# One product of the v projection cut into token pieces in three retention heads, and a scalar projection with 64 weight columns

## What is computed

```python
h = rmsnorm(x, norm_mix_w[i])
# layer 0: four retention heads and four gated-delta heads in parallel
rq, rk, rv, rg, qkv, gz, ga, gb = _split(h @ w_in, HYB_SIZES)
rv = sw(rv.astype(jnp.float32).reshape(Bsz, L, RET_HEADS, RET_DV))
ro, ret_s = ret_fn(rq, rk, rv, log_gamma, ret_s0)
g = -jnp.exp(a_log) * jax.nn.softplus(ga + dt_bias)
beta = jax.nn.sigmoid(gb)
go, gdn_s = gdn_fn(gq, gk, gv, sw(g), sw(beta), gdn_s0)
x = x + mixed @ w_out
# layer 1: a Mamba-2 state-space mixer; each layer is followed by a SwiGLU
x = x + swiglu(rmsnorm(x, norm_ffn_w[i]), wg, wu, wd)
```

## Time and profile before

| | |
|---|---|
| three runs | 3317.96, 3323.27, 3329.45 us |
| median | 3323.27 us |
| span of the profiled execution | 3317.2 us |
| TensorE busy, matmul / weight load | 3143.7 us (95%) / 3030.1 us (91%), 20090 of each |
| DVE, ScalarE, GpSimd busy | 1775.8, 799.8, 1019.1 us |
| mean granted TensorE clock | 0.986 of full speed |

### The profile page before, as it was taken

The page is one execution under the profiler, slowest core; times in us unless marked ns, Lnnn a source line. Parts: engine busy times, 40 slices in busy tenths (PEclk is TensorE's granted clock), DMA queues, the critical chain, the costliest instruction groups (busy, mean ns, idle before and its releaser), DMA issues. The chain is left out here.

```text
span 3317.2 us, 46817 instructions
## 1 busy us (share of the span) xinstructions
PE 3143.7 (95%) x20090; PEld 3030.1 (91%) x20090; DVE 1775.8 (54%) x2023; ACT 799.8 (24%) x1176; POOL 1019.1 (31%) x528
## 2 busy tenths in 40 slices
PE   6999899998899999999989998999988999999997
PEld 5899898888799999999988897989978999999997
DVE  5344657566543333333487869678696333333335
ACT  4222414324420000000145415243253000000002
POOL 2222201111023333333334536345362333333331
PEclk9999999999899999999999999999999999999999
DMA  4111100101011111111113214132231111111111
GB/s 147 59 71 59 49 26 33 40 26 40 21 44 45 50 46 45 45 51 45 45 42 121 86 58 148 62 118 74 82 128 37 51 45 45 50 47 45 46 51 64
DMA packets 94474, 198.15 MB, mean 60 GB/s; under 512 B 21796, under 2 KB 52164, under 8 KB 94152
## 3 DMA queue, kind: packets, MB, share of 16 engines
q1 hardware_dynamic: 52384, 150.03, 12.9%
q10 hardware_dynamic: 41896, 45.23, 4.3%
HBM read 171.41 MB, written 19.59 MB: 58 GB/s over the span
## 5 line engine op out<-in xcount | busy, mean ns | idle before, releaser
L492 POOL CAST w_hi<-w_raw 128x1024 fp32r<-128x1024 f32 x230 | 256.8, 1116 | 2181.2 <-PE ps_set L565 1971.5
L565 PE MATMUL ps_set<-h_hi,w_hi 128*128 128x344 f32 x3648 | 806.0, 329 | 2.2 <-DVE work L2179 1.3
L565 PE MATMUL ps_set<-h_lo,w_hi 128*128 128x344 f32 x3648 | 776.8, 321 | 0.0
L565 PE MATMUL ps_set<-h_hi,w_lo 128*128 128x344 f32 x3648 | 772.0, 320 | 0.0
L565 PEld LDWEIGHTS ps_set<-h_hi,w_hi 128*128 128x128 f32 x3648 | 615.5, 189 | 26.8 <-issue 18.7
L565 PEld LDWEIGHTS ps_set<-h_lo,w_hi 128*128 128x128 f32 x3648 | 619.9, 190 | 0.0
L565 PEld LDWEIGHTS ps_set<-h_hi,w_lo 128*128 128x128 f32 x3648 | 610.6, 188 | 0.0
L495 POOL TENSOR_TENSOR w_lo<-w_raw,w_hi 128x1024 fp32r<-128x1024 f32 x230 | 599.0, 2605 | 18.4
L1824 DVE TENSOR_TENSOR x<-x,ps_set 128x1032 f32<-128x1032 f32 x160 | 196.7, 1229 | 255.6 <-PE ps_set L565 255.6
L1131 ACT ACTIVATE work<-work 128x1032 f32<-128x1032 f32 (+5 forms) x190 | 180.7, 959 | 496.0 <-DVE work L2179 447.9
L565 PE MATMUL ps_set<-y_hi,w_hi 128*128 128x344 f32 x1296 | 282.7, 327 | 8.5 <-DVE y_lo L2360 7.0
(11 more groups left out here) (229 smaller groups left out, 3652.7 us busy)
## 6 DMA issues: line engine op xcount, KB each, us to landing
w_raw<-in_w SPq DMA_DIRECT2D x230, 512.0 KB, 3.2
work<-ssm_cum_rows ACTq DMA_DIRECT2D x32, 512.0 KB, 4.8
sample<-in_ssm_state SPq DMA_DIRECT2D x16, 512.0 KB, 5.1
out_ssm_s<-sample SPq DMA_DIRECT2D x16, 512.0 KB, 2.8
x<-in_x SPq DMA_DIRECT2D x6, 688.0 KB, 15.5
work<-work ACTq DMA_DIRECT2D x16, 258.0 KB, 2.4
out_y<-x SPq DMA_DIRECT2D x6, 688.0 KB, 3.4
sample<-bc_rows SPq DMA_DIRECT2D x8, 512.0 KB, 4.7
```

The source lines that it names most:

```text
L492: return nc.gpsimd.tensor_copy(w_hi[:, k, :], w_raw[:, k, :])
L565: mm = nc.tensor.matmul(out[:, g, 0:TN], w[:, slot, cols], v[:, g * TN:(g + 1) * TN], start=(start and n == 0), stop=(stop and n == 2))
```

## The change

`split_products` gets two arguments: `m`, the number of weight columns loaded (and of output partitions written), and `cuts`, the ends of the pieces into which each token group of the second product (`n == 1`, high weight x low activation) is cut. `slices` and `tile` pass them on. The v projection is called with other cuts for each head: head 0 with the whole 344, head 1 with 258 and 86 tokens, head 2 with 172 and 172, head 3 with 86 and 258. The scalar projection of layer 0 is called with `m` = 64. All other calls keep their 128 columns and one piece.

```diff
-            def split_products(out, slot, block, rhs, start, stop):
+            def split_products(out, slot, block, rhs, start, stop, m=P, cuts=(TN,)):
 
                 hi, lo = rhs
-                cols = slice(block * P, block * P + P)
+                cols = slice(block * P, block * P + m)
                 for n, (w, v) in enumerate(((w_hi, hi), (w_hi, lo), (w_lo, hi))):
                     for g in range(TG):
-                        mm = nc.tensor.matmul(out[:, g, 0:TN], w[:, slot, cols], v[:, g * TN:(g + 1) * TN],
-                                              start=(start and n == 0), stop=(stop and n == 2))
+                        first = 0
+                        for last in cuts if n == 1 else (TN,):
+                            mm = nc.tensor.matmul(out[0:m, g, first:last], w[:, slot, cols], v[:, g * TN + first:g * TN + last],
+                                                  start=(start and n == 0), stop=(stop and n == 2))
+                            first = last
                 return mm
...
-                fill(project("v", h), KC)
+                fill(slices(big_, f"v.{h}", 0, RET_UNIT["v", h], RET_UNIT["v", h], P, ((TN,), (258, TN), (172, TN), (86, TN))[h]), KC)
...
-            tile(big_jobs["gdns"], "sc", 0, GDNS, GDNS)
+            tile(big_jobs["gdns"], "sc", 0, GDNS, GDNS, 64)
```

More of the change, by code:

```diff
@@ L628, in pair_outputs, with slices @@
                 mm.then_inc(*((unit_done, 1) if done else (part_done, 1)))
-            def slices(jobs, job, turn, unit, slot):
+            def slices(jobs, job, turn, unit, slot, m=P, cuts=(TN,)):
                 part = take(jobs, job, turn)
@@ L636, in slices @@
                 for c in range(KC):
-                    mm = split_products(ps_set[part], slot % 2, c, (h_hi[:, c, :], h_lo[:, c, :]), c == 0, c == KC - 1)
+                    mm = split_products(ps_set[part], slot % 2, c, (h_hi[:, c, :], h_lo[:, c, :]), c == 0, c == KC - 1, m, cuts)
                     if c == KC - 1:
@@ L640, in slices, with tile @@
                     yield
-            def tile(jobs, job, turn, unit, slot):
-                for _ in slices(jobs, job, turn, unit, slot):
+            def tile(jobs, job, turn, unit, slot, m=P):
+                for _ in slices(jobs, job, turn, unit, slot, m):
                     pass
```

## The result

The changed kernel takes 3327.89 us (median of 20 runs, 3322.65 to 3336.48), the kernel before 3323.01 us beside it (20 runs, 3315.6 to 3329.45). The ratio is 1.0016, with a 95% interval of 1.0009 to 1.0023: 4.9 us slower by the medians and 5.3 us by the ratio (interval 3.0 to 7.6 us), where 5.3 us were forecast. It is within 0.3%, and clear of zero only because of the twenty runs.

What follows compares the result with a forecast made beforehand. TensorE was taken to bound the kernel, with matmuls under way 95% of the span. Splits of 1.85 + 1.63 + 1.85 = 5.3 us plus zero for the scalar projection took the median 3323.27 to 3328.6 us; range 3318 to 3339.

Steps and rivals of the forecast that it cites:

- the three stretches: v projections of heads 1, 2 and 3, 72 matmuls each: forecast to last 13.2, 13.0, 13.2 us instead of 11.4.
- The windows in which the prediction looked: The last 11.4 us before 142.5, 217.5 and 292.5 us, taken as v of heads 1 to 3, TensorE full.
- The count: v of heads 1 to 3: 24 further matmuls and 24 further loads a head, 72 in all, same moving columns.
- The floor of 113 ns: Short v pieces: each costs at least 113 ns, set by the load of 128 weight columns.
- the surcharge: 14.5 ns above the pure stream of 143.3 ns for 344 columns, added to each piece's streaming time.
- the prediction's own sign: v of heads 1 and 3: equal stretches would show that the order of long and short pieces means nothing.
- The scalar projection: 72 matmuls loading 64 weight columns: priced at zero, at most 1.0 us of gain or loss.
- Pieces at the float32 rate: Rival at the v pieces: 86 columns cost 228 ns, 172 cost 292 ns; 19.4 us slower together, chance 0.09.
- The fixed price of 157.8 ns: Rival at the v pieces: every float32r matmul takes 157.8 ns however few its columns; 11.4 us slower, chance 0.07.
- No floor: Rival at the v pieces: the second load hides or is left out, 1.0 us remains, 3324.3 us; chance 0.10.
- The clock: Rival: shifted low-clock stretches give over 10 us gain, chance 0.03; clock falling inside v stretches, up to 34 us, chance 0.01.
- nothing absorbs it: After v in heads 1 to 3: no later wait takes up the 5.3 us, so all of it reaches the path.

Runs made afterwards that it cites:

- v_quarters: The changed kernel with the second product of v in heads 1 and 3 cut into four 86-column pieces: 3338.51 us against 3322.38 before, ratio 1.0053.
- v_half_loads: The changed kernel with all v projections loading 64 weight columns, upper 64 rows omitted: v stretches 11.30, 11.82, 11.35, 11.76 us (heads 0 to 3), one execution.

## Why the prediction was right

**The bound and the place.** TensorE set the end, and in the three stretches nothing else was near. The 5.13 us that the stretches grew by are the 4.9 us of the medians within the interval (3.0 to 7.6 us). The windows in which the prediction looked were about 1.3 us late: v of head 1 runs from 129.80 to 141.17, and what follows up to 142.5 is the slice of the g projection, likewise in heads 2 and 3. TensorE is as full in one as in the other, so nothing hung on it. The DVE rotation that the k transposes need was ready as early as foreseen; the row after that answers to the earlier trace rows has the last operation at 214.49, and the transposes at 222.2.

```profile
214.49 1.23 DVE L1892 TENSOR_TENSOR work<-work 128x1032 f32<-128x1032 f32 x1
```

**The count** of 72 matmuls and 72 loads is in the page.

**The price.** The floor of 113 ns, read from float32 rows of 1 and of 128 columns, holds for float32r too: 112 ns in v_quarters. The forecast of 77, 68 and 77 ns a split stands against 77, 65 and 72. The small miss is in the surcharge, which the prediction added as 14.5 ns to every piece whatever its width, where nearly all of it goes with the columns. By 0.459 ns a column (157.8 ns for 344) the 258-column piece is 118 ns, not 122, and 118 + 112 - 158 = 72 ns is what head 3 shows. For 172 columns nothing changes by it; with 112 ns for the floor and 158 for the whole the sum is 66, measured 65. That head 1 agrees with its forecast is partly luck, since that forecast has the same 4 ns too much in it. By the prediction's own sign the order of a long and a short piece means something: head 1, with its long piece ahead, pays 5 ns more a split than head 3. Why was not tried.

**No slack is passed on.** The prediction took the larger of stream and load for each piece and added then, without a reason; adding first and comparing then would have given another price. The runs bear it out. The pieces of head 3 stream for 39 + 118 ns, together the 158 of the whole, and their two loads take 224; had the long piece made good what the short one lacks, a split would cost 224 - 158 = 66 ns there as in head 2. It costs 72. The single starts in the trace show where the wait falls: from an 86-column piece to the start of the next 258-column one it is only 40 ns, and from that to the next 190, which is its own 118 and the 72 that the short one lacked.

**The scalar projection** was priced at zero between +1.0 and -1.0 us. It gave 0.13 to 0.15 us (11.30 and 11.28 us against 11.43): about 0.1 us by 1.2 to 1.4 ns a matmul, and the rest in the first slice.

**The rivals.** Pieces at the float32 rate would have shown 290 ns a piece of 172 columns; head 2's have 112 (a slice of 1.62 us), and so have the pieces of 86 in v_quarters, where the prediction's rival had 228. The fixed price of 157.8 ns falls with the same rows. No floor falls with the 5.1 us; what would take the floor away is shorter loads, as v_half_loads shows. The Trainium skill's rule for the isolated distance, columns / 2.4 + 2.5 ns ("TensorE: Matmul & The Clock Gate", section "Back-to-back issue gap"), would give 38 ns for 86 columns; they took 112 with full loads and 58 with half, and the section itself says that in a stream of loads and matmuls the spacing is set by both. Its section "LDWEIGHTS", columns / 1.2, gives 107 and 53 ns for a load. The distances from start to start agree to about 5 ns; the durations of the load rows, 190 and 135 ns, do not.

**The clock** did move low stretches about, worth 5.1 us in the state-space stage of a single profile, and nothing in the medians beyond their interval.

**One step that held for this place only.** The prediction's "nothing absorbs it" was argued from the waits of the three heads. Where TensorE has waits that a longer projection can fill it doesn't hold: a quarter of the price did not show in the state-space stage (20.5 of 83.2 us).

No experiment pointed to a version faster than before that computes the whole result: the load is already hidden under 344 columns, and the narrow load gives 0.15 us where it can be had.

## What to carry to other kernels

A matmul costs the larger of its stream and of the load of its weights, and here each one loads anew, even with the same weights. Take the larger for each matmul and add then: a long neighbour does not make good what a short one lacks. For 128 columns the load is 112 ns, that is the stream of about 245 columns of float32r at 2.4 GHz; cut no piece shorter than that unless it loads fewer columns too. Read what a short matmul costs over a whole slice, not from the row it stands in, since its wait falls behind its successor. An isolated count times such a floor is a good price only where TensorE hardly waits; in a stage where it waits for other engines between its projections, part of the price disappears.

## What was not expected of the hardware

The float32r stream runs at 0.459 ns a column at the upper clock, 10% above 0.417, nearly in proportion to the width (157 ns for 344, 80 for 172), and without the surplus at the lower clock. Less than a tenth of the surplus goes away with half the weight load beside it. Float32 matmuls of 344 columns (L660, L585) start every 288 or 289 ns at the upper clock in the kernel before: two cycles a column are 287, so they show almost no surplus either.
